# A two-part decoder on one core: first-block order of rounding, squares, tables, group merges and turned memory rows

## The chip, the cores and the metric

One NeuronCore of a Trainium2 chip runs the whole program. The metric is the device time of one execution in microseconds; the median of three runs of the kernel before is 2056.19 us (2055.5 to 2057.44). Five engines work side by side: TensorE (matmuls, PE in the rows; its weight loads are PEld), VectorE (DVE), ScalarE (ACT), GpSimd (POOL) and SyncE (SP), which issues most transfers. They meet only at semaphores.

## What is computed

256 tokens of width 1024, all in float32, pass through a first part of two blocks and a second part of four layers. The change lies in the first part and at the first layer of the second. Cut to what matters:

```python
for l in range(2):                                   # first part
    h = rms_norm(x, norm_gain[l])
    cols = h @ w_in[l]                               # 1024 -> many columns
    if l == 0:   # three groups of dilated attention (8 heads each), merged by softmax of their log-denominators
        q, k = rotary(rms_norm(q) * q_gain, cos, sin), rotary(rms_norm(k) * k_gain, cos, sin)
        alpha = softmax(stack([lse0, lse1, lse2]))
        mix = sum(alpha[g] * out[g] for g in range(3))
    else:        # gated linear scan with lower bounds from a softmax over lb_logits
        mix = hgrn2(cols, lower_bounds)
    kv = rms_norm(mem, mem_gain[l]) @ w_mem_kv[l]    # 256 memory rows, 4 heads
    mem_out = softmax(q_mem @ k_mem.T * scale) @ v_mem
    x = x + (concat([mix, mem_out]) * silu(gate)) @ w_out[l]
# second part: gated linear attention, latent attention, convolution, gated linear attention;
# the latent attention uses rotary tables of its own (other positions), each layer has an MLP and a gate
```

## The kernel before

`plan()` writes the whole order of work out by hand as a list of steps (`add(kind, ...)`), and `build()` walks that list once for each engine. So each engine executes its share of every step in the order of the list, and a step that waits holds up all that stands behind it on that engine.

**Weights** come as units of 128 x 2048 floats (1 MB), numbered in the order of use, through a ring of four slots. SyncE issues unit n when the subtraction of unit n - 4 is done (L862 to L864), the constants being issued ahead of unit 4. For float32 accuracy each unit is split in two: ScalarE writes `whi`, a rounded copy (L1256), VectorE writes `wlo` = raw - whi (L1563). TensorE multiplies three times (L908): hi x hi, hi x lo, lo x hi. ScalarE's copy runs three units ahead of the use, VectorE's subtraction two. A projection to 512 columns takes two units and 48 matmuls of 512 columns.

**Turned rows.** TensorE turns four 128 x 128 tiles into a bank (L1084), ScalarE writes the rounded copy (L1376), VectorE the rest (L2049), which frees the bank. There are two such banks. The products need the turned rows of h (X) or of y and of the memory (Y) as their other operand.

**First block.** Units 0 and 1 give the values of the memory, 2 and 3 its keys, 4 and 5 the memory's queries; then six times v, q and k of four heads (units 6 to 41), three groups for each half `hq` of the heads; units 42 to 47 are the gates, 48 to 53 the output product with its six chunks of rows (u = 0 to 5: 0 and 1 need heads 0 to 3, 2 and 3 heads 4 to 7, 4 and 5 the memory's part of y). After a projection of q or k ScalarE squares and copies both banks (L1298, L1265), VectorE reduces, takes the root and multiplies with scale and gain (L1666 to L1675), and turns by the angles (L1691 to L1702). The four heads of a quad go through a pipeline of slots between projections: T (turn q and k, L1005; copy by ScalarE, L1403), S (scores, L1026; mask and maximum on VectorE, L1842; exponential on ScalarE, L1410), PT (turn, L1034; copy L1856), PV (L1049; copy L1866). `combine` computes the weights of the three groups and then merges their outputs: 8 multiplications (L2105) and 16 multiply-adds (L2109). `ymul` (L2122) multiplies a chunk of y with its gate. `memgain` (`gained`, L1627) multiplies the memory rows by their gain, `xnorm` (`norm`) normalises x for the second block. `init` computes the rotary tables of the first block and the lower bounds, `mlatab` (L2191 to L2199) those of the latent attention; both need a sine or an exponential of ScalarE.

**Second block.** Units 54 and 55 are the memory's values, 56 and 57 its keys, 58 and 59 its queries, 60 onwards the second block's own projections. X holds the turned memory rows up to unit 57 and the turned x from unit 58.

The order of the steps around the change, as `plan()` has it before:

```python
add("memgain", layer=0); turn_x("mg", "Y"); add("first_units"); add("scales", what="mem")
...  # values, keys, queries of the memory: units 0 to 5
add("init"); add("mlatab")
...  # six rounds of v, q, k; combine(hq=0) after the fifth; the gates with turns of y; drain()
```

## Time and profile before

| what | us |
|---|---|
| median of three runs | 2056.19 |
| the profiled execution | 2057.1 |
| its span | 2055.3 |
| TensorE busy in it | 1908.8 |
| VectorE busy | 1207.5 |
| ScalarE busy | 910.0 |
| GpSimd busy | 593.1 |

The span is the time from the first to the last instruction of the profiled execution; the rest of its time lies around it. A row of the timeline gives the start in us, the length in us, the engine, the line, the operation, what it writes and reads, how many instructions are merged in it, and in brackets the idle time of the engine before it and who ended it.

### The profile page before, as it was taken

How to read it: one execution, taken by the hardware profiler on the slowest of the kernel's cores; microseconds unless marked ns; L12 is line 12 of the kernel's file. 1: busy time of each engine (PE TensorE's matmuls, PEld its weight loads, DVE VectorE, ACT ScalarE, POOL GpSimd, SP SyncE). 2: the span in 40 equal slices, each digit the busy share in tenths (PEclk: the TensorE clock that was granted, in tenths of full speed). 3: DMA queues.
4: the chain of work that ended last, by engine and by line, in shares of the span. 5: the costliest groups of instructions: out<-in, count | busy, mean ns of one | idle time of the engine just before them, and what ended most of it. 6: DMA issues, size and time to landing. Idle time of an engine off the chain costs nothing.

```text
span 2055.3 us, 27371 instructions
## 1 busy us (share of the span) xinstructions
PE 1908.8 (93%) x11072; PEld 1678.5 (82%) x11072; DVE 1207.5 (59%) x2062; ACT 910.0 (44%) x981; POOL 593.1 (29%) x132
## 2 busy tenths in 40 slices
PE   6899989989888988999989999999999988989998
PEld 5688877779777877899778899889899977779996
DVE  6788787775977397332566522566522376863236
ACT  5555545345443343444354444443444434334442
POOL 0000000000000001787400688500487700037870
PEclk9999999999899999999999999999999999999999
DMA  7344434534332234455443455444655533164551
GB/s 291 123 145 143 178 130 144 195 142 150 103 124 97 110 117 155 164 198 190 145 162 137 182 179 192 183 156 163 221 180 188 186 124 140 62 222 171 189 199 44
DMA packets 53412, 324.94 MB, mean 158 GB/s; under 512 B 8480, under 2 KB 11936, under 8 KB 16064
## 3 DMA queue, kind: packets, MB, share of 16 engines
q1 hardware_dynamic: 45344, 310.10, 41.4%
q10 hardware_dynamic: 7968, 13.44, 2.0%
q8 instruction: 70, 1.15, 0.2%
q14 instruction: 30, 0.25, 0.0%
HBM read 322.47 MB, written 1.05 MB: 157 GB/s over the span
## 4 chain that ended last, share of the span: by engine, by line
PE 73%; DVE 20%; ACT 4%; issue 2%; DMA 0%; SPq 0%; DVEq 0%; ACTq 0%
PE project L908 41%; PE output L908 25%; DVE wlo L1563 3%; PE turn L1084 1%; ACT whi L1256 1%; DVE XTl L2049 1%; PE output L1026 1%; PE output L1049 1%; DVE arena L1675 1%; DVE tok L2257 1%; DVE arena L1901 1%; DVE arena L1903 1%; DVE arena L1927 1%; ACT XTh L1376 1%; PE turn L1005 1%
## 5 line engine op out<-in xcount | busy, mean ns | idle before, releaser
L876 POOL TENSOR_TENSOR wlo<-raw,whi 128x2048 fp32r<-128x2048 f32 x128 | 592.9, 4660 | 1415.0 <-ACT whi L1256 1398.1
L1256 ACT ACTIVATE whi<-raw 128x2048 fp32r<-128x2048 f32 x291 | 554.4, 1913 | 477.3 <-PE project L908 308.4
L908 PE MATMUL project<-XTh,whi 128*128 128x256 f32 x1488 | 427.0, 287 | 4.4 <-DVE XTl L2049 3.0
L908 PE MATMUL project<-XTh,wlo 128*128 128x256 f32 x1488 | 425.0, 286 | 0.0
L908 PE MATMUL project<-XTl,whi 128*128 128x256 f32 x1488 | 424.9, 286 | 0.0
L2285 DVE TENSOR_TENSOR arena<-arena 128x512 f32<-128x512 f32 x64 | 143.2, 2271 | 462.0 <-ACT arena L1513 462.0
L1563 DVE TENSOR_TENSOR wlo<-raw,whi 128x2048 fp32r<-128x2048 f32 x163 | 376.6, 2323 | 39.0 <-ACT whi L1256 38.7
L908 PE MATMUL output<-whi,YTh 128*128 128x512 f32 x736 | 291.7, 396 | 13.2 <-DVE YTl L2049 11.4
L908 PEld LDWEIGHTS project<-XTh,whi 128*128 128x128 f32 x1488 | 290.0, 195 | 7.4 <-DVE XTl L2049 4.9
L908 PEld LDWEIGHTS project<-XTh,wlo 128*128 128x128 f32 x1488 | 289.9, 195 | 1.0
L908 PEld LDWEIGHTS project<-XTl,whi 128*128 128x128 f32 x1488 | 289.6, 195 | 0.0
L908 PE MATMUL output<-wlo,YTh 128*128 128x512 f32 x736 | 289.6, 393 | 0.0
L908 PE MATMUL output<-whi,YTl 128*128 128x512 f32 x736 | 289.1, 393 | 0.0
L908 PE MATMUL project<-whi,XTh 128*128 128x512 f32 x624 | 256.2, 411 | 12.7 <-DVE wlo L1563 9.3
L908 PE MATMUL project<-whi,XTl 128*128 128x512 f32 x624 | 246.0, 394 | 0.0
L908 PE MATMUL project<-wlo,XTh 128*128 128x512 f32 x624 | 246.0, 394 | 0.0
L908 PEld LDWEIGHTS output<-whi,YTh 128*128 128x128 f32 x736 | 140.2, 190 | 42.5 <-DVE YTl L2049 12.0
L908 PEld LDWEIGHTS output<-whi,YTl 128*128 128x128 f32 x736 | 139.9, 190 | 30.0
L908 PEld LDWEIGHTS output<-wlo,YTh 128*128 128x128 f32 x736 | 140.1, 190 | 27.6
L908 PEld LDWEIGHTS project<-whi,XTh 128*128 128x128 f32 x624 | 119.4, 191 | 41.5 <-DVE wlo L1563 12.3
L908 PEld LDWEIGHTS project<-whi,XTl 128*128 128x128 f32 x624 | 118.9, 190 | 26.3
L908 PEld LDWEIGHTS project<-wlo,XTh 128*128 128x128 f32 x624 | 119.4, 191 | 23.6
(245 smaller groups left out, 2104.7 us busy)
## 6 DMA issues: line engine op xcount, KB each, us to landing
raw<-in_units SPq DMA_DIRECT2D x291, 1024.0 KB, 4.8
arena<-in_ln_g ACTq DMA_DIRECT2D x8, 512.0 KB, 4.1
arena<-in_ln_b ACTq DMA_DIRECT2D x8, 512.0 KB, 4.9
arena<-in_mem_norm_gain ACTq DMA_DIRECT2D x2, 512.0 KB, 4.9
...
xres<-in_x SPq DMA_DIRECT2D x1, 1024.0 KB, 12.9
arena<-in_mem ACTq DMA_DIRECT2D x1, 1024.0 KB, 6.6
...
```

The costliest lines, as they stand in the source:

```text
L876: pool.tensor_tensor(wlo[:, slot, :], raw[:, slot, :], whi[:, slot, :], ALU.subtract).then_inc(lo_pool, 1)
L908: mm = pe.matmul(out, x if x_stationary else w, w if x_stationary else x, start=start and i == 0, stop=stop and i == 2, skip_group_check=True)
L1005: mm = pe.transpose(PT[hd["t"] % 2][:, x * P:(x + 1) * P], buf[:, h, jj * P:(jj + 1) * P], ident[:, :])
L1026: mm = pe.matmul(PQ[h2][:, h * S:h * S + n], qkT[:, h2, h * P:(h + 1) * P], qkT[:, h2, S:S + n], start=True, stop=True)
L1049: mm = pe.matmul(PQ[3][:, h * P:(h + 1) * P], pT[:, h2, x * P:(x + 1) * P], v, start=kt == 0, stop=kt == len(mine) - 1)
L1084: mm = pe.transpose(PT[f["t"] % 2][:, x * P:(x + 1) * P], s, ident[:, :])
L1256: act.activation(whi[:, slot, :], raw[:, slot, :], ACT.Copy).then_inc(hi_done, 1)
L1376: act.activation(dst[:, f["k"]:f["k"] + nk, f["h"] * P:(f["h"] + 1) * P], PT[t % 2][:, 0:nk * P].rearrange("p (k t) -> p k t", k=nk), ACT. ...
L1563: dve.tensor_tensor(wlo[:, slot, :], raw[:, slot, :], whi[:, slot, :], ALU.subtract).then_inc(lo_dve, 1)
L1675: ins = dve.scalar_tensor_tensor(out=v, in0=v, scalar=st[:, 24 + x:25 + x], in1=gain, op0=ALU.mult, op1=ALU.mult)
L1901: dve.tensor_tensor(QE[l % 2], q, Dx, ALU.mult).then_inc(dve_own, 1)
L2285: dve.tensor_tensor(hsq[:, b, :], relu[:, b, :], relu[:, b, :], ALU.mult).then_inc(hsq_ready, 1)
```

## The change

- The rounding of unit 0 stands between the two pairs of turns of the memory rows, those of units 1 and 2 and both subtractions behind them; the squares of the memory rows come after, and their scales within the first projection.
- `init` keeps the first block's tables and stands before the projection of the memory's queries. The lower bounds are a step `floors` of their own, before the memory keys of the second block. `mlatab` moves into the first projection of the second part, with the loads of its positions and constants, now on ScalarE's queue.
- `combine` keeps the weights only. The merges are steps `merge(hq, g)`: for hq = 0 groups 0 and 1 after the first unit of the last v projection, group 2 after the first unit of the last q projection; for hq = 1 between the units of the output product, whose order becomes 4, 5, 0, 1, 2, 3.
- The turns of y's chunk 0 move from inside the last gate projection to behind it.
- The gain multiplication of the memory rows (layer 1) comes after unit u = 1 of the output product, and their turns stand in two pairs before and between the halves of its tail (which is split into x = 0, 1 and x = 2, 3).
- `xnorm` stands between the two units of the second block's value projection, and the turns of x are split: the first four tiles of both halves between the key projection's units, the others behind it.
- In a slot ScalarE does the stage T before the others.

The diff, cut to what the text speaks of:

```diff
+            if xs[0] == 0:
+                units.extend((w, "Q", v, 0) for v in (u, u + 1))
+            m = len(units) - 2
+            add("tail", n=m, ahead=False, **f)
+            add("ahead", n=m + (xs[0] > 0), on="sv")
...
     add("memgain", layer=0)
-    turn_x("mg", "Y")
-    add("first_units")
-    add("scales", what="mem")
-    vg = project(("w_mem_kv", 0), 512, "v", src="M", par=0, between=lambda: add("xgain"))
+    turn("mg", 0, 0, "Y", 0)
+    turn("mg", 0, 1, "Y", 4)
+    add("first_units", s=(0,), v=())
+    turn("mg", 1, 0, "Y", 0)
+    turn("mg", 1, 1, "Y", 4, late=True)
+    add("first_units", s=(1, 2), v=(0, 1))
+    add("squares", what="mem")
+    vg = project(("w_mem_kv", 0), 512, "v", src="M", par=0,
+                 between=lambda: (add("scales", what="mem"), add("xgain")))
...
     project(("w_mem_kv", 0), 0, "qk", src="M", gain=7, rot=False, dst="k", between=lambda: turn_tok_half(1))
+    add("init")
     project(("w_in_a", 0), 9216, "qk", gain=6, rot=False, dst="q")
-    add("init")
-    add("mlatab")
     quad("mem", vg, par=0, g=3)
...
     for hq in range(2):
         for g in range(3):
             col = g * 1024 + hq * 512
-            vg = project(("w_in_a", 0), 6144 + col, "v", par=par)
-            project(("w_in_a", 0), col, "qk", gain=g, rot=True, dst="q")
+            last = hq == 1 and g == 2
+            vg = project(("w_in_a", 0), 6144 + col, "v", par=par, between=(lambda: merge(0, 0, 1)) if last else None)
+            project(("w_in_a", 0), col, "qk", gain=g, rot=True, dst="q", between=(lambda: merge(0, 2)) if last else None)
             project(("w_in_a", 0), 3072 + col, "qk", gain=3 + g, rot=True, dst="k")
...
     project(("w_in_a", 0), 9728, "gate", buf="A", between=lambda: turn_y(2))
     add("ymul", chunk=0, layer=0, second=0)
-    project(("w_in_a", 0), 9728 + 512, "gate", buf="A", between=lambda: turn_y(0))
+    project(("w_in_a", 0), 9728 + 512, "gate", buf="A")
+    for h in range(H2):
+        turn("y", h, 0, "Y", 0, late=True)
     drain()
 
     g, one, tail = begin_output(("w_out_a", 0), 1536)
     add("combine", hq=1, quads=(4, 5, 6))
+    add("load", what="mem")
+    one(4, first=True)
+    merge(1, 0, 1)
+    one(5)
+    merge(1, 2)
     add("ymul", chunk=1, layer=0, second=0)
-    add("load", what="mem")
-    one(0, first=True)
-    add("memgain", layer=1)
-    one(1)
-    one(4)
+    one(0, whole=True)
     for h in range(H2):
         turn("y", h, 1, "Y", 4, late=True)
     add("load", what="b")
-    one(5)
-    tail(2)
-
-
-    turn_x("tok", "X")
+    one(1)
+    add("memgain", layer=1)
+    turn("tok", 0, 0, "X", 0)
+    turn("tok", 0, 1, "X", 4)
+    tail(2, 0, 1)
+    turn("tok", 1, 0, "X", 0)
+    turn("tok", 1, 1, "X", 4)
+    tail(2, 2, 3)
+
     add("qpost", g=g, post="resid", src_n=n["src"])
-    add("xnorm", layer=1)
-    vg = project(("w_mem_kv", 1), 512, "v", par=2)
-
-    def turn_tok():
-        turn_x("tok", "X")
-
-    project(("w_mem_kv", 1), 0, "qk", gain=1, rot=False, dst="k", before_vector=turn_tok)
+    vg = project(("w_mem_kv", 1), 512, "v", par=2, between=lambda: add("xnorm", layer=1))
+
+    def turn_tok(c):
+        turn("tok", 0, c, "X", 4 * c, late=c == 1)
+        turn("tok", 1, c, "X", 4 * c, late=c == 1, later=1 - c)
+
+    add("floors")
+    project(("w_mem_kv", 1), 0, "qk", gain=1, rot=False, dst="k", between=lambda: turn_tok(0),
+            before_vector=lambda: turn_tok(1))
...
-        project(w, 0, "fq", feature_major=True, scale=SCALE, second=1)
+        project(w, 0, "fq", feature_major=True, scale=SCALE, second=1, between=(lambda: add("mlatab")) if j == 0 else None)
...
+                if j == 0:
+                    load(posM.bitcast(I32), a["pos_row"].to_broadcast([P, S]), pos_in)
+                    load(small, a["c_small"], pos_in)
...
                 elif kind == "first_units":
-                    for n in range(AHEAD):
+                    for n in f["s"]:
                         hi(n, n, 1)
...
-                    for stage, i in f["stages"]:
+                    for stage, i in sorted(f["stages"], key=lambda x: x[0] != "T"):
...
+                elif kind == "merge":
+
+                    g = f["g"]
+                    dve.wait_ge(*last.at)
+                    for j in range(4):
+                        for h in range(H2):
+                            y = yA[:, h, (4 * f["hq"] + j) * P:(4 * f["hq"] + j + 1) * P]
+                            s = st[:, 32 + 8 * g + 2 * j + h:33 + 8 * g + 2 * j + h]
+                            if g == 0:
+                                dve.tensor_scalar(y, y, s, None, ALU.mult).then_inc(dve_own, 1)
+                                last.own()
+                            else:
+                                o = tok[:, g - 1, h * 512 + j * P:h * 512 + (j + 1) * P]
+                                dve.scalar_tensor_tensor(out=y, in0=o, scalar=s, in1=y, op0=ALU.mult, op1=ALU.add).then_inc(dve_own, 1)
+                                last.own()
+                    dve.wait_ge(*last.at)
                 elif kind == "ymul":
```

## Rows read from the trace of the kernel before

**Rows 1.** Page, chain that ended last: shares of the span by engine.
```profile
PE 73%; DVE 20%; ACT 4%; issue 2%; DMA 0%; SPq 0%; DVEq 0%; ACTq 0%
```

**Rows 2.** Timeline of TensorE, first 460 us: rows after long stops.
```profile
19.49 0.76 PE L908 MATMUL project<-whi,YTh 128*128 128x512 f32 x1 [4.90 <-DVE wlo L1563]
...
76.91 2.07 PE L1026 MATMUL output<-arena 128*128 128x256 f32 x4 [8.63 <-ACT arena L1403]
...
297.70 0.80 PE L908 MATMUL project<-whi,XTh 128*128 128x512 f32 x1 [4.75 <-DVE wlo L1563]
...
350.80 0.63 PE L1084 MATMUL turn<-ident,arena 128*128 128x128 f32 x4 [2.09 <-ACT arena L1403]
...
376.40 0.94 PE L1049 MATMUL output<-arena 128*128 128x128 f32 x6 [1.30 <-DVE arena L1856]
...
390.08 0.50 PE L908 MATMUL output<-whi,YTh 128*128 128x512 f32 x1 [1.82 <-DVE wlo L1563]
```

**Rows 3.** Windows of 24 matmuls, TensorE: window, length, busy (count), granted clock, DMA, GB/s.
```profile
78.98:86.09 7.11, 7.11 (x27) 0.77 0.79 303
87.83:93.33 5.50, 5.50 (x27) 1.00 0.20 48
...
351.43:358.53 7.10, 7.10 (x26) 0.76 0.37 113
```

**Rows 4.** Start: unit 0's transfer (issue to landing), then timelines of three engines.
```profile
raw<-in_units SPq DMA_DIRECT2D x1, 1024.0 KB, 8.1
...
15.12 3.70 ACT L1256 ACTIVATE whi<-raw 128x2048 fp32r<-128x2048 f32 x2
...
21.25 56.80 SPq L864 DMA_DIRECT2D raw<-in_units  x10
...
30.54 1.92 ACT L1256 ACTIVATE whi<-raw 128x2048 fp32r<-128x2048 f32 x1 [5.00 <-DMA raw<-in_units]
...
45.63 0.69 ACT L1298 ACTIVATE arena<-project,st 128x512 f32<-128x512 f32 x1 [1.39 <-PE project L908]
...
51.40 4.49 DVE L1563 TENSOR_TENSOR wlo<-raw,whi 128x2048 fp32r<-128x2048 f32 x2
```

**Rows 5.** Timeline of VectorE and ScalarE, tables and bounds.
```profile
62.28 0.16 DVE L1971 CAST st<-st 128x2 f32<-128x2 int32 x1
...
65.09 0.26 ACT L1362 ACTIVATE arena<-arena 128x64 f32<-128x64 f32 x1 [4.21 <-DVE arena L1616]
65.36 1.28 ACT L1366 ACT_TABLE_LOAD   x1
66.66 0.22 ACT L1366 ACTIVATE lbs<-lbs 128x16 f32<-128x16 f32 x1
...
67.63 0.29 DVE L2191 CAST arena<-arena 128x256 f32<-128x256 int32 x1
...
72.81 0.35 DVE L2199 TENSOR_SCALAR csM<-csM,arena 128x256 f32<-128x256 f32 x1 [0.70 <-ACT csM L1370]
```

**Rows 6.** Timeline of VectorE, first merge and what follows.
```profile
289.21 1.66 DVE L2105 TENSOR_SCALAR arena<-arena,st 128x128 f32<-128x128 f32 x8
290.90 4.42 DVE L2109 SCALAR_TENSOR_TENSOR arena<-tok,st,arena 128x128 f32<-128x128 f32 x16
...
305.63 0.56 DVE L1856 COPY arena<-output 128x384 f32<-128x384 f32 x1 [2.51 <-PE output L1034]
...
312.88 0.42 DVE L1866 COPY tok<-output 128x256 f32<-128x256 f32 x1 [3.54 <-PE output L1049]
```

**Rows 7.** Second part's start: a small load (issue to landing), then timelines.
```profile
arena<-in_gla_glr ACTq DMA_DIRECT2D x1, 64.0 KB, 2.3
...
690.12 0.60 ACT L1265 ACTIVATE arena<-project 128x512 f32<-128x512 f32 x1 [7.79 <-PE project L908]
...
695.63 0.49 DVE L2146 TENSOR_TENSOR YTl<-arena,YTh 128x128 fp32r<-128x128 f32 x2 [10.94 <-ACT YTh L1453]
```

**Rows 8.** Timeline of ScalarE, a slot of the gate stage.
```profile
349.19 0.40 ACT L1410 ACTIVATE arena<-arena,negm 128x128 f32<-128x128 f32 x1 [3.43 <-DVE negm L1848]
...
350.08 0.57 ACT L1403 ACTIVATE arena<-turn 128x512 f32<-128x512 f32 x1
```

**Rows 9.** TensorE's waits, 400 to 460 us (total, times, longest); then VectorE's timeline.
```profile
PE turn L1084 <- DVE XTl L2049: 3.1, 2, 1.8
PE project L908 <- DVE XTl L2049: 1.6, 2, 0.8
PE project L908 <- DVE wlo L1563: 1.5, 1, 1.5
...
443.01 1.29 DVE L2049 TENSOR_TENSOR XTl<-turn,XTh 128x512 fp32r<-128x512 f32 x2 [8.65 <-ACT XTh L1376]
...
454.19 4.49 DVE L1563 TENSOR_TENSOR wlo<-raw,whi 128x2048 fp32r<-128x2048 f32 x2
```

44 lines of the change are left out of this document (19 added, 25 removed).

## The prediction

> **What bounds the kernel now.** I read three views in this order. The chain that ended last gives TensorE 73% of the span and VectorE 20% [rows 1]: the time is TensorE's own work plus the places where it stands still. The timeline of TensorE with its idle times, read over the first 460 us (all that the diff touches but the angle tables of the second part), gives those places [rows 2]. The granted clock over equal groups of work gives the second part of the price: 24 matmuls take 5.50 us at 1.00 (2.4 GHz), and 7.10 and 7.11 us where the clock over them averages 0.76 and 0.77, so part of them ran at 1.2 GHz [rows 3]. The slow group is the one right after the stop of 2.09 us; the stops of 8.63 and 4.75 us are followed by such groups too, and the first matmul after 4.75 us takes 0.80 us, after 1.82 us only 0.50 [rows 2]. So a long stop costs its own length plus 1.6 us, a short one its own length.
>
> I number the 1 MB weight units as the kernel does. Each needs a rounding copy on ScalarE (1.9 us [rows 4]) and a subtraction on VectorE (2.3 us [rows 9]) before TensorE may use it.
>
> **The start.** TensorE begins at 19.49 [rows 2]. Before that ScalarE does two squares in front of the turned tiles, and unit 0's rounding starts only at 15.12, though its transfer landed 8.1 us after its issue at 2.1, so at 10.2 [rows 4]. The change rounds unit 0 between the two pairs of turns. Working forward: turned copies until 9.7, rounding 10.2 to 12.1, second pair of copies to 13.3, the rests on VectorE to 14.1, then unit 0's subtraction to 16.4. TensorE would begin about 3.0 us earlier. But 13.4 us later it wants the value bank freed, by a ScalarE copy that stands in the queue behind the rounding of unit 4. That rounding waited 5.00 us for its transfer and ran from 30.54 [rows 4]. The constants ahead of unit 4 on the SP queue stay, except one of 128 KB, some 0.4 us. The copy thus ends near 32.6, and TensorE goes on at 32.65 where before it went on at 33.5. **The 3.0 us shrink to 0.85.** The stop that takes their place is about 1.9 us, between the one of 1.82 without and the one of 2.09 with a lowered clock; I take it as without and keep 1.6 us for the range.
>
> **Tables out of the way.** Now VectorE does both tables and the bounds in one run from 62.28 to 73.2, ScalarE waits 4.21 us and then again for it [rows 5], the roundings and TensorE stand behind, and TensorE stops 8.63 us [rows 2]. The change puts only the first table ahead of the projection of q. It is 2.8 us on VectorE (62.28 to 65.09 [rows 5]) plus 0.35 us for the sine. Queued behind it: on VectorE unit 6's subtraction; on ScalarE, which waits for VectorE's angles, unit 7's rounding and then the square and copy of q's first bank. The k projection ends at 45.6 now, where ScalarE takes up its square [rows 4], and would end at 44.75. From there: 5.9 us to the end of VectorE's normalisation (as now, 45.6 to 51.5, the next subtraction from 51.40 [rows 4]), 2.8 table, 0.35 sine, 1.9 rounding, 1.3 square and copy, which is 56.95. Unit 6 began at 56.51 before, so this point is 0.45 us *later* and the start's gain is used up. What is late next: q's normalisation ends near 64, just before its first turn at 65.2. I find no further wait. Gain here: 8.63, plus 1.0 for the four score matmuls after the stop (2.07 us [rows 2], half of it at the full clock), plus 1.6 for the next 24, less 0.45: **10.8 us**.
>
> Each sine also switches ScalarE's table: 1.28 us, and the load starts before the wait, under cover. The rows show nothing after the load: the one at 65.36 ends at 66.64 and the exponential runs from 66.66 [rows 5]. The Trainium skill, *ScalarE: Activation LUTs*, section "What ACT_TABLE_LOAD costs", puts a switch at about 2.66 us, with a drain of 1.38 us. By that the first block would lose another 1.4 us at unit 7's rounding; the rest of the sum goes without it.
>
> **Second table.** It moves into the first projection of the first gated layer of the second part, behind one subtraction. VectorE needs 5.5 us for it (67.63 to 73.16 [rows 5]) where it sat idle 10.94 us [rows 7]; ScalarE, which would wait about 4.3 us for it, is idle there 7.79 us until the next bank is full, 690.12 [rows 7]. Queued behind on VectorE is one subtraction, needed some 7 us later. Nothing on the path: 0. Its two transfers go out on ScalarE's queue, about 0.45 us each, before a rounding that waits for TensorE in any case. If the cover were gone it would cost at most 5.5 us. The bounds' own step (about 2.2 us, after unit 57's subtraction) has unit 58's subtraction behind it, due more than 5 us later: 0.
>
> **First merge in pieces.** Now 6.1 us of merges (1.66 and 4.42 [rows 6]) stand before unit 38's subtraction, and TensorE stops 4.75 us [rows 2]. The weights' own chain (about 2.4 us ahead of 289.21) stays. With the merges moved, unit 38 is ready at 291.5, before its use at 292.95. Then VectorE does 3.9 us of merge, unit 39, and only at 298.0 the scores that TensorE finished at 292.5. Their exponential ends at 299.7; TensorE, through with unit 38 at 298.4, and with a turn, wants it at 298.75. **New wait 1.0 us**, without a loss of clock. The remaining 2.2 us go behind the next scores. VectorE's two idle stretches here, 2.51 and 3.54 us [rows 6], are together as long as the merges, so unit 42 finds nothing late. Gain: 4.75 + 1.6 - 1.0 = **5.4 us**.
>
> **Turned copy ahead of the exponential.** In the gate stage TensorE waits 2.09 us [rows 2] for a turned copy at 350.08, which stands behind an exponential that waited for VectorE [rows 8]. The turn itself was over by 347.3. Taking it first ends that stop and its slow group: 2.09 + 1.6 = **3.7 us**. In the other slots it changes the order of two ScalarE steps that nobody waits for: 0.
>
> **The output product and the second memory block.** Here stand 1.30 and 1.82 us [rows 2], 3.1 and 1.6 (two stops of each kind, around the turned rows) and 1.5 us [rows 9], 9.3 together. The first shrinks to about 0.5, as the turns of y now run while VectorE copies. Chunks 4 and 5 go first, so unit 50's subtraction comes behind the weights' chain alone: 5 us early. The merges (3.9, 2.2) and the gate product (1.4) end at about 388, one microsecond before the turn of chunk 1. The memory rows are then turned between products, where TensorE has 5.5 us of other matmuls after each pair; their gain multiplications end 0.6 us before they are wanted, the narrowest cover in this stage. The norm's 7.5 us run beside the value projection. The second turning is split by halves, so the rests of the first pair are done under unit 57. New is this: from the k projection's end to unit 60's subtraction it takes 13.4 us (1.9 to the first rest, and from 443.01 to 454.19 less one pair, plus 2.3 [rows 9]), while TensorE has only one pair of turns and two units, 11.9 us. **Wait 1.5 us** at unit 60. Gain: 9.3 - 0.5 - 1.5 = 7.3, and some 0.6 us for six restarts of the matmul pipe: **7.9 us**.
>
> **The sum.** 10.8 + 5.4 + 3.7 + 7.9 = 27.8 us. The profiled execution has a span of 2055.3 and a time of 2057.1, so 1.8 us lie around the span; it would become 2027.5 and 2029.3. The median of the runs shown, 2056.19, is 0.9 below the profiled one: **2028.4 us**, a ratio of 0.986. After unit 60 nothing on the path is changed.
>
> **The rivals.** *(a) The new short waits lower the clock, or VectorE becomes the bound.* TensorE now arrives earlier at places where VectorE works without a pause. Three new stops (1.9 at the value bank, 1.0 at unit 38's scores, 1.5 at unit 60) with 1.6 us each cost 4.8 us more: 2033.2. For it: the first of them is near 2 us. Against: the stop of 1.82 us. *(b) The start's gain survives.* If unit 4 lands earlier because its slot is asked for earlier, up to 2.1 us more come through, and unit 6 moves along since its chain hangs on the k projection: 2026.3. Against: the SP queue issues unit 4 at 21.25 [rows 4], after its constants, and not when slot 0 came free at 19.3. *(c) The merges come back.* If the merges in the g2 projections hold up q's or k's normalisation by their whole length, the first merge's 5.4 us are lost and no more: 2033.8. *(d) Slower than before:* the position row and the small constants now land late. VectorE's angles wait for them, the next subtraction stands behind, and TensorE wants that unit about 697. A landing before 690 costs nothing; each microsecond after that costs one, so 34 us late (724) makes the kernel slower by 0.2%. Its issue is near 662 and the first of the other small loads there landed after 2.3 us [rows 7], so I give it almost nothing. *(e) It doesn't do what it says:* if TensorE's stops are only moved, as where VectorE's total work sets the time, the gain is that of the tables alone, 11 us: 2045. Against it: VectorE's idle stretches stand beside the stages concerned [rows 6, 7].
>
> **Chances.** Forecast 0.62, (a) 0.14, (b) 0.08, (c) 0.08, (e) 0.04, a loss that I don't see but still faster 0.01, no change 0.015, slower 0.015 ((d) among it). The range 2022.5 to 2034.5 takes in (a), (b) and (c) with the unknown ends: 2.5 us for the two new waits if they don't come, and as much again for stops that I have mis-sized. Less than 0.2% (4 us) can't be told from no change here; faster 0.97, same 0.015, slower 0.015.
>
> **What would show it.** Right: TensorE's first matmul near 16.5 and a stop of some 2 us near 31; unit 6 near 57; no stop at 68 to 77 and scores near 69; a stop of 1 us instead of 4.75 after unit 38; none before the turns of y; one of 1.5 us at unit 60; granted clock 1.00 after each. Wrong: a stop over 2 us in any of these with a group at 0.8, a stop in the first gated layer near 660, or a difference in the spacing of the second part.

## The result and the profile after

The changed kernel takes **2029.45 us** (median of four runs, 2026.15 to 2030.73) beside 2056.82 us for the kernel before in the same session (2055.5 to 2057.9). The ratio is 0.9865, with a 95% interval from 0.9848 to 0.9882. The forecast was 2028.4 within 2022.5 to 2034.5. The profiled execution has a span of 2028.9 us and a time of 2030.67.

The first 460 us of TensorE's timeline show nearly all of it. Columns are start, length, engine, line, operation, and in brackets the idle time before the row with what ended it. Lines of the changed kernel are 27 to 33 higher in this region (L908 is now L935, L1563 is L1593). It answers [rows 2].

```profile
16.31 0.76 PE L935 MATMUL project<-whi,YTh 128*128 128x512 f32 x1 [4.54 <-DVE wlo L1593]
...
31.46 0.47 PE L935 MATMUL project<-whi,YTh 128*128 128x512 f32 x1 [0.57 <-ACT arena L1292]
...
55.49 0.47 PE L935 MATMUL project<-whi,XTh 128*128 128x512 f32 x1 [1.09 <-ACT arena L1292]
...
98.66 0.47 PE L935 MATMUL project<-whi,XTh 128*128 128x512 f32 x1 [0.47 <-ACT arena L1292]
...
287.66 0.55 PE L1061 MATMUL output<-ident,arena 128*128 128x128 f32 x3 [1.13 <-ACT arena L1440]
...
354.21 0.94 PE L1076 MATMUL output<-arena 128*128 128x128 f32 x6 [0.43 <-DVE arena L1886]
...
409.36 0.47 PE L935 MATMUL project<-whi,XTh 128*128 128x512 f32 x1 [1.62 <-DVE XTl L2079]
...
428.27 0.50 PE L935 MATMUL project<-whi,XTh 128*128 128x512 f32 x1 [1.43 <-DVE wlo L1593]
```

The stops of 8.63, 4.75, 2.09 and 1.82 us are gone. What stands there now is short, and no slow group follows: the first matmul behind each stop at a weight unit takes 0.47 to 0.50 us, not 0.80. The granted clock over the stretches that begin at these stops is 1.00, where [rows 3] had 0.77 and 0.76 (columns as there).

```profile
31.46:37.00 5.54, 5.54 (x24) 1.00 0.59 231
...
67.41:71.00 3.59, 3.59 (x18) 1.00 1.01 420
287.66:293.00 5.34, 5.34 (x26) 1.00 0.93 370
...
409.36:415.00 5.64, 5.64 (x25) 1.00 0.32 135
428.27:434.00 5.73, 5.73 (x25) 1.00 0.80 296
```

Then something goes the other way. I use two marks in the code that the change left alone: the first turn in the scan of the second block (the last chunk's, the "scan turn" below), and the first matmul of the eighth scan level. Between them the changed kernel takes 43.1 us and the kernel before 39.2. First the changed kernel:

```profile
492.91 1.97 PE L1111 MATMUL turn<-ident,arena 128*128 128x128 f32 x8 [3.11 <-DVE arena L2155]
...
536.04 1.16 PE L1170 MATMUL output<-arena 128*128 128x128 f32 x8 [1.40 <-DVE arena L1938]
```

and the kernel before:

```profile
521.42 1.26 PE L1084 MATMUL turn<-ident,arena 128*128 128x128 f32 x8 [3.10 <-DVE arena L2122]
...
560.63 2.08 PE L1143 MATMUL output<-arena 128*128 128x128 f32 x8 [1.40 <-DVE arena L1908]
```

So in these two profiles the gain is 28.5 us at the scan turn (521.42 - 492.91), 24.6 at the eighth level, and 26.4 at the end of the span (2055.3 - 2028.9). Is the loss of 3.9 us a price of the change, or does it come from elsewhere? That became the main question for the experiments, next to the forecast's own terms.

### The profile page after: what moved, and what is told of

It is laid out like the page before. It is cut to its first block, busy times and chain, and to the rows that moved or that the text cites. A ratio compares the mean times of both kernels' runs of the same rounds, so it can differ in the third digit from the quotient of the medians.

```text
span 2028.9 us, 27379 instructions
## 1 busy us (share of the span) xinstructions
PE 1907.0 (94%) x11072; PEld 1679.5 (83%) x11072; DVE 1206.5 (59%) x2062; ACT 910.5 (45%) x981; POOL 593.2 (29%) x132
## 4 chain that ended last, share of the span: by engine, by line
PE 73%; DVE 20%; ACT 3%; issue 3%; SPq 1%; DMA 0%; DVEq 0%; ACTq 0%
PE project L935 40%; PE output L935 26%; DVE wlo L1593 3%; PE turn L1111 1%; ACT whi L1283 1%; DVE XTl L2079 1%; DVE arena L1705 1%; DVE tok L2290 1%; PE output L1076 1%; SPq L866 1%; PE output L1053 1%; DVE arena L1931 1%; DVE arena L1933 1%; DVE arena L1957 1%; DVE st L2272 1%
## 5 line engine op out<-in xcount | busy, mean ns | idle before, releaser
L935 PE MATMUL project<-XTh,whi 128*128 128x256 f32 x1488 | 426.4, 287 | 4.1 <-DVE XTl L2079 3.1
L935 PE MATMUL project<-XTh,wlo 128*128 128x256 f32 x1488 | 424.4, 285 | 0.0
L935 PE MATMUL project<-XTl,whi 128*128 128x256 f32 x1488 | 424.2, 285 | 0.0
L1593 DVE TENSOR_TENSOR wlo<-raw,whi 128x2048 fp32r<-128x2048 f32 x163 | 376.9, 2322 | 38.8 <-ACT whi L1283 38.0
L935 PE MATMUL output<-whi,YTh 128*128 128x512 f32 x736 | 291.4, 396 | 11.4 <-DVE YTl L2079 11.4
L935 PEld LDWEIGHTS project<-XTh,whi 128*128 128x128 f32 x1488 | 289.3, 194 | 7.2 <-DVE XTl L2079 4.9
L935 PEld LDWEIGHTS project<-XTh,wlo 128*128 128x128 f32 x1488 | 289.1, 194 | 1.0
L935 PE MATMUL output<-wlo,YTh 128*128 128x512 f32 x736 | 289.2, 393 | 0.0
L935 PEld LDWEIGHTS project<-XTl,whi 128*128 128x128 f32 x1488 | 288.9, 194 | 0.0
L935 PE MATMUL output<-whi,YTl 128*128 128x512 f32 x736 | 288.9, 392 | 0.0
L935 PE MATMUL project<-whi,XTh 128*128 128x512 f32 x624 | 255.1, 409 | 8.9 <-DVE wlo L1593 4.5
L935 PE MATMUL project<-whi,XTl 128*128 128x512 f32 x624 | 245.4, 393 | 0.0
L935 PE MATMUL project<-wlo,XTh 128*128 128x512 f32 x624 | 244.9, 392 | 0.0
L935 PEld LDWEIGHTS output<-whi,YTh 128*128 128x128 f32 x736 | 140.2, 190 | 39.9 <-DVE YTl L2079 12.0
L935 PEld LDWEIGHTS output<-whi,YTl 128*128 128x128 f32 x736 | 139.7, 190 | 29.8
L935 PEld LDWEIGHTS output<-wlo,YTh 128*128 128x128 f32 x736 | 140.0, 190 | 27.6
L935 PEld LDWEIGHTS project<-whi,XTh 128*128 128x128 f32 x624 | 118.9, 191 | 37.1 <-DVE wlo L1593 8.5
L935 PEld LDWEIGHTS project<-whi,XTl 128*128 128x128 f32 x624 | 118.2, 189 | 26.0
L935 PEld LDWEIGHTS project<-wlo,XTh 128*128 128x128 f32 x624 | 118.7, 190 | 23.3
```

The costliest lines, as they stand in the source:

```text
L935: mm = pe.matmul(out, x if x_stationary else w, w if x_stationary else x, start=start and i == 0, stop=stop and i == 2, skip_group_check=True)
L1593: dve.tensor_tensor(wlo[:, slot, :], raw[:, slot, :], whi[:, slot, :], ALU.subtract).then_inc(lo_dve, 1)
```

## The experiments

The first four kernels ran together, then the next four, then the last four; the kernel before ran beside them each time (2056.36, 2056.86 and 2056.66 us). Two theories stand over all of them for the lost 3.9 us. **A**: the moments at which TensorE's clock falls and comes back around the scan turn differ by chance. **B**: the change, by its timing or its order, keeps the clock low.

### The changed kernel again

No edit.

> The changed kernel once more, unaltered. It asks about the first scan levels of the second block: from the first turn of y's third chunk (492.9) to the eighth level's matmuls (536.0) the profiled changed kernel takes 43.1 us, the kernel before 39.2 us, although nothing there was edited. Theory A (chance: after the stops there the clock comes back at another moment in each execution): another execution gives another length, between 39 and 44, and single times spread over some 4 us. Theory B (the change itself lowers the clock there, by arriving at it in another state): 43 again, within 0.5. Everything up to unit 60 (428.3) repeats within 0.3 us in either case.

Measured: 2029.47 us (2024.19 to 2030.23), ratio 0.9861 [0.9845, 0.9878]. Unit 60 at 428.4, scan turn at 493.02, from there to the eighth level 42.9 us. The single length spoke for B, though the four times spread over 6 us, which theory A had expected (some 4 us).

### The old start

```diff
-    turn("mg", 0, 0, "Y", 0)
-    turn("mg", 0, 1, "Y", 4)
-    add("first_units", s=(0,), v=())
-    turn("mg", 1, 0, "Y", 0)
-    turn("mg", 1, 1, "Y", 4, late=True)
-    add("first_units", s=(1, 2), v=(0, 1))
     add("squares", what="mem")
+    turn_x("mg", "Y")
+    add("first_units", s=(0, 1, 2), v=(0, 1))
+    add("scales", what="mem")
```

> The changed kernel with the start of before: squares ahead of the turned copies, all three roundings behind them, the scales ahead of the first projection. Theory (the start is limited by unit 4's transfer, and its gain reaches unit 6 because that unit hangs on the end of the memory's k projection): first matmul at 19.5 in place of 16.3, but unit 2 at 33.5 in place of 31.5 and unit 6 at 57.5 in place of 55.5: 2.0 us of the 3.2 come through, unit 60 at 430.3. Rival (as I predicted: only 0.85 comes through): unit 2 at 32.3, unit 60 at 429.1. Rival 2 (all comes through): unit 60 at 431.5. Time about 2 us over the changed kernel.

Measured: 2029.43 us (2026.55 to 2031.76), ratio 0.9872 [0.9856, 0.9889]. The first matmul is back at 19.61, unit 2 starts at 33.97, unit 6 at 58.00, unit 60 at 430.85 and the scan turn is at 495.50, 2.4 us later than in the mean of the changed kernel's four profiles (493.1). That lies between the theory (2.0) and rival 2 (all 3.2); the rival (0.85) is out. Yet the median is the same; in the profiled execution the stretch behind the scan turn takes 39.1 us. A median of four runs can't show what the start is worth. The trace can. It also shows why my forecast of the start was too low. Three timelines, of ScalarE's rounding of unit 4, in the changed kernel, in this one, and in the next (old tables), whose position row is back on the SP queue:

```profile
28.83 1.92 ACT L1283 ACTIVATE whi<-raw 128x2048 fp32r<-128x2048 f32 x1 [1.90 <-DMA raw<-in_units]
```

```profile
28.93 1.92 ACT L1279 ACTIVATE whi<-raw 128x2048 fp32r<-128x2048 f32 x1 [3.27 <-DMA raw<-in_units]
```

```profile
20.89 0.43 SPq L867 DMA_DIRECT2D arena<-in_pos_row  x1
21.37 21.69 SPq L893 DMA_DIRECT2D raw<-in_units  x6
...
29.76 1.91 ACT L1285 ACTIVATE whi<-raw 128x2048 fp32r<-128x2048 f32 x1 [2.72 <-DMA raw<-in_units]
```

With the old start but without the row, unit 4 is ready at 28.93, as early as with the new start. With the new start and the row it is ready at 29.76, and in the two profiles of the kernel before (old start and row) at 30.54 [rows 4] and 30.39. Over the eleven profiles without the row this start lies between 28.76 and 29.18. So the row on the queue costs 0.6 to 1.0 us of landing with the new start (29.76 against 28.76 to 29.18), and 1.5 to 1.6 with the old one (30.39 and 30.54 against 28.93), though its issue takes only 0.43 us. The traffic shows it too: from 24 to 26 us the transfers move 153 GB/s in this one profile with the new start and the row and 186 and 192 in the kernel before, but 269 to 330 in all profiles without the row. Without the row the moment at which slot 0 comes free plays no part (28.93 against 28.83). Why it costs more with the old start stays open.

### The old tables and bounds

```diff
-    add("init")
     project(("w_in_a", 0), 9216, "qk", gain=6, rot=False, dst="q")
+    add("init")
+    add("floors")
+    add("mlatab")
...
+                load(posM.bitcast(I32), a["pos_row"].to_broadcast([P, S]), pos_in)
```

(Not shown: at their new places `floors`, `mlatab` and the two small loads go.)

> The changed kernel with both tables and the bounds again behind the projection of the memory's queries, and the loads as before. Theory (the stop is the price, all else stays): TensorE stops 8.6 us before the first scores of memory, then runs a group of 24 at a clock under 0.8; 8.6 + 1.0 + 1.6 less the 1.1 us stop at unit 6 = 10.1 us more at unit 12 (98.7 to 108.8) and at unit 60 (428.3 to 438.4). Rival (later stops of VectorE absorb part of it, since it could work ahead during the stop): under 6 us at unit 60. The first layer of the second part shows no difference in either.

Measured: 2041.73 us (2040.74 to 2042.16), ratio 0.9929 [0.9912, 0.9945]. TensorE's timeline has the long stop back:

```profile
75.78 2.08 PE L1055 MATMUL output<-arena 128*128 128x256 f32 x4 [8.61 <-ACT arena L1432]
...
109.46 0.47 PE L937 MATMUL project<-whi,XTh 128*128 128x512 f32 x1 [0.50 <-ACT arena L1294]
```

Unit 12 starts at 109.46 and not at 98.66: 10.8 us, up to 0.9 of them from the row's effect on unit 4 (unit 2 starts at 32.40 and not at 31.46). The expectation was 10.1; the rival, under 6, is out. The stop's clock is in it. The windows from 75.78 to 80.00 and from 80.00 to 84.00 show 0.50 and 0.94, and 1.00 behind. The scan turn is 10.6 us later (503.70), and the stretch behind it takes 41.6 us, a value between the two seen so far. What the first gated layer of the second part shows is told below, at the second table.

### The old first merge

```diff
-            vg = project(("w_in_a", 0), 6144 + col, "v", par=par, between=(lambda: merge(0, 0, 1)) if last else None)
-            project(("w_in_a", 0), col, "qk", gain=g, rot=True, dst="q", between=(lambda: merge(0, 2)) if last else None)
+            vg = project(("w_in_a", 0), 6144 + col, "v", par=par)
+            project(("w_in_a", 0), col, "qk", gain=g, rot=True, dst="q")
...
+                merge(0, 0, 1, 2)
```

> The changed kernel with the three merges of the first half back in one piece behind their weights. Theory: the stop of 4.75 us ahead of unit 38 and its slow group come back and the stops of 0.23 and 1.13 us go: unit 42 5.1 us later (310.5 to 315.6), unit 60 the same 5.1 us later (433.4). Rival (VectorE's whole work bounds this stretch, so that the merges cost their 6.1 us wherever they stand): under 2 us.

Measured: 2033.87 us (2031.19 to 2036.16), ratio 0.9887 [0.987, 0.9903]. The stop is back, the new one of 1.13 is not there:

```profile
285.60 0.79 PE L936 MATMUL project<-whi,XTh 128*128 128x512 f32 x1 [4.96 <-DVE wlo L1594]
```

Unit 42 starts at 316.53 and not at 310.48, 6.05 us later: 4.96 less 1.13 is 3.8 of them. I put the remaining 2.2 down to the clock, which stood at 0.50 over the 4.4 us from 285.60. The expectation was 5.1; the rival, under 2, is out. The scan turn is 5.9 later (498.98), the stretch behind it 42.9.

### Turned copies in the old order

```diff
-                    for stage, i in sorted(f["stages"], key=lambda x: x[0] != "T"):
+                    for stage, i in f["stages"]:
```

> The changed kernel, with the turned copy of attention's result no longer taken first among the copies of an output group: ScalarE copies in the order in which the pieces stand, as before the change. Forecast by the prediction's step (turned copy first, 3.7): TensorE's stop of about 2.1 us at the first transpose of the attention rows comes back, with the slower group of matmuls behind it at a granted clock below 1.00, and unit 57 and unit 60 start 3.7 us later than in the changed kernel (409.4 and 428.3 there); median about 3.5 later. Rival: the copy was late only because of the merges, which now stand elsewhere; then the stop stays gone and the times are those of the changed kernel within 0.5. On the clock in the second block's scan levels (turn of chunk 2 to level 8, 43 us in the changed kernel, 39 with the start undone): theory A, it depends on when the stop falls and not on the change: any value between 39 and 44; theory B, the change's later parts cause it: 43.

Measured: 2032.98 us (2031.27 to 2034.98), ratio 0.9889 [0.9871, 0.9907]. The stop of 2.09 is back:

```profile
333.99 0.63 PE L1111 MATMUL turn<-ident,arena 128*128 128x128 f32 x4 [2.09 <-ACT arena L1433]
```

But the slow group is not. TensorE's window behind it:

```profile
334.00:350.00 16.00, 16.00 (x86) 1.00 0.32 109
```

The same stop, to the hundredth of a microsecond, had a clock of 0.76 behind it in [rows 3], and a lowered one in the second profile of the kernel before too (0.68 over the first 4 us). So its price is 2.1 us and a restart, or 1.6 more with the slow group, and which of them is paid is not a matter of the stop's length. With one profile of this kernel, whether chance or something else in the order decides at this stop isn't shown. From unit 42 to the output product this kernel takes 46.75 us and the changed kernel 44.4, so undoing the order costs 2.3 here. Units 57 and 60 are 2.9 us later (3.7 expected), the scan turn 2.7 (495.83), some 0.4 of it from before unit 42. The rival (no stop) is out. The stretch behind the scan turn takes 39.1 us.

### The old order of the output product

```diff
-    one(4, first=True)
-    merge(1, 0, 1)
-    one(5)
-    merge(1, 2)
+    merge(1, 0, 1, 2)
     add("ymul", chunk=1, layer=0, second=0)
     one(0, whole=True)
+    one(4, first=True)
...
-    turn("tok", 0, 0, "X", 0)
-    turn("tok", 0, 1, "X", 4)
-    tail(2, 0, 1)
-    turn("tok", 1, 0, "X", 0)
-    turn("tok", 1, 1, "X", 4)
-    tail(2, 2, 3)
+    one(5)
+    tail(2)
+    turn_x("tok", "X")
```

(Not shown: the turns of y and the second load now stand between chunks 1 and 5. The order of the chunks is 4, 0, 1, 5, where the kernel before had 0, 1, 4, 5, so this is near the old order and not the same. The turns of y's chunk 0 stay behind the last gate projection here; no run moves them back.)

> The changed kernel with the output product and its memory rows scheduled as before the change: the last merge in one piece, token groups 4, 0, 1, 5 in the old order, the tail whole, and the turns of the memory block's rows behind all of it. Forecast by the prediction's step (9.3 removed less 0.5 and 1.5 of new waits and 0.6 kept, for this and for the second block's order together): TensorE's stops of 1.8, 1.3 and 0.5 us in the output product come back, unit 57's stop of 1.62 us goes since nothing turned is still on its way, and the normalisation stands in front of the value projection. Unit 60 starts 4 to 6 us later than in the changed kernel (428.3), so near 433; median 4 to 5 later. Rival: the three stops came from the merges in one piece of the first block alone, and the order in the output product is worth under 1.5 us. On the clock in the second block's scan levels: theory A any value between 39 and 44 us; theory B 39, since the turns that the change put in front are gone.

Measured: 2036.97 us (2035.69 to 2039.85), ratio 0.9906 [0.9887, 0.9926]. TensorE's timeline:

```profile
368.17 0.50 PE L929 MATMUL output<-whi,YTh 128*128 128x512 f32 x1 [2.12 <-DVE wlo L1587]
...
393.36 1.23 PE L1105 MATMUL turn<-ident,tok 128*128 128x128 f32 x8 [1.35 <-DVE XTl L2073]
395.40 0.79 PE L929 MATMUL project<-whi,XTh 128*128 128x512 f32 x1 [0.81 <-DVE XTl L2073]
...
415.93 0.47 PE L929 MATMUL project<-whi,XTh 128*128 128x512 f32 x1 [1.62 <-DVE XTl L2073]
...
434.84 0.50 PE L929 MATMUL project<-whi,XTh 128*128 128x512 f32 x1 [1.44 <-DVE wlo L1587]
```

Unit 60 is 6.6 us later (434.84), a little above the expected 4 to 6; the scan turn 6.4. The stops shown ahead of unit 57 sum to 4.3 us. Another 1.4 is the clock behind the pair of 1.35 and 0.81, 0.57 over 4 us:

```profile
395.00:399.00 4.00, 3.60 (x10) 0.57 0.00 0
```

From 395.40 the next 24 matmuls take 6.98 us; behind the same pair in the first profile of the kernel before (at 417.34) they take 5.58 us, and in the second profile of the kernel before 7.02. I had expected the 1.3 us ahead of the output product (376.40 in [rows 2]) back, and it stayed at 0.43: that gain is not this order's, and the move of the turns of y's chunk 0, which stays, is what the prediction gave it to. I had expected unit 57's 1.62 us to go, and it did not. It belongs to the order of the second memory block and not to the output product. The stretch behind the scan turn takes 39.2 us.

### The old order of the second memory block

```diff
-    vg = project(("w_mem_kv", 1), 512, "v", par=2, between=lambda: add("xnorm", layer=1))
+    add("xnorm", layer=1)
+    vg = project(("w_mem_kv", 1), 512, "v", par=2)
...
-    project(("w_mem_kv", 1), 0, "qk", gain=1, rot=False, dst="k", between=lambda: turn_tok(0),
-            before_vector=lambda: turn_tok(1))
+    project(("w_mem_kv", 1), 0, "qk", gain=1, rot=False, dst="k", before_vector=lambda: turn_x("tok", "X"))
```

> The changed kernel with the second memory block in the old order: the normalisation of the memory rows ahead of the value projection, and all turns of the token rows behind the key projection. The output product stays as the change has it. Forecast: of the two stops that the changed kernel shows there (1.62 us at unit 57 for a turned copy, 1.43 at unit 60 for a rounded half) both go or shrink, and those of before at the key projection and at the turns (1.5, 1.6, 0.8) come back; unit 60's counterpart, the first query unit, starts 1.0 to 1.6 us later than 428.3. Rival: VectorE has the same work ahead of unit 57 whichever way it is ordered, so the sum is the same within 0.5 us.

Measured: 2029.43 us (2027.36 to 2032.92), ratio 0.9865 [0.9847, 0.9883]. The two stops of the changed kernel go, and the two around the turned rows come back, 2.61 us in place of 3.05. The third that I expected, 1.5 us at unit 56 [rows 9], does not, so its removal is not this part's work:

```profile
415.28 1.22 PE L1107 MATMUL turn<-ident,tok 128*128 128x128 f32 x8 [1.79 <-DVE XTl L2075]
417.32 0.79 PE L931 MATMUL project<-whi,XTh 128*128 128x512 f32 x1 [0.82 <-DVE XTl L2075]
```

By its stops the old order is 0.4 us better, not 1.0 to 1.6 worse. But here the clock falls behind them, as the windows show:

```profile
415.00:419.00 4.00, 2.90 (x12) 0.68 0.00 0
419.00:423.00 4.00, 4.00 (x10) 0.50 0.45 137
423.00:427.00 4.00, 4.00 (x18) 0.97 0.30 125
```

That costs some 2.8 us (2.4 later at the next common unit in spite of 0.4 less of stops), so the scan turn is 2.5 us late (495.61). In the kernel before, the same pair of stops at 443.85 and 445.89 had a clock of 1.00 on both sides. So this part of the change is worth nothing by its stops, and some 3 us in executions in which the clock falls behind the old ones. It did so in this one profile and in neither of the two of the kernel before. The stretch behind the scan turn takes 42.9 us.

### Two waits removed: units 57 and 59

The changed kernel's stop at 409.36 is not one of those I forecast. The profile shows what is wrong with it. VectorE's timeline in the changed kernel around it:

```profile
404.73 2.29 DVE L1593 TENSOR_TENSOR wlo<-raw,whi 128x2048 fp32r<-128x2048 f32 x1
407.97 1.29 DVE L2079 TENSOR_TENSOR XTl<-turn,XTh 128x512 fp32r<-128x512 f32 x2 [0.95 <-ACT XTh L1406]
...
416.90 1.29 DVE L2079 TENSOR_TENSOR XTl<-turn,XTh 128x512 fp32r<-128x512 f32 x2 [7.64 <-ACT XTh L1406]
```

TensorE waits until 409.36 for rests of the tiles 0 to 3, which the code turned just before; unit 57 itself reads tiles 4 to 7. The wait comes from `wait_turned`, which waits for every turned pair in flight unless it is marked `late`, and this pair is not (`late=c == 1`). And VectorE then stands idle for 7.64 us, and does the rests of the next pair ahead of unit 59's subtraction although both could wait in the other order.

```diff
                 elif kind == "proj":
-                    wait_turned("Y" if f["src"] == "M" else "X", whole=f["u"] == 1)
+                    if f["n"] != 57:
+                        wait_turned("Y" if f["src"] == "M" else "X", whole=f["u"] == 1)
...
         if before_vector is not None:
+            add("ahead", n=m, on="v")
             before_vector()
         if tag in ("qk", "fq"):
-            add("ahead", n=m, on="sv")
+            add("ahead", n=m, on="s" if before_vector is not None else "sv")
```

> The changed kernel with two waits removed by their cause. First, unit 57 (the first value unit of the second memory block) no longer waits for the turned pair of tiles 0 to 3: it reads tiles 4 to 7 alone, and that pair's copies are waited for by the unit that reads them. Second, the subtraction that makes unit 59's low half of its weights goes to VectorE ahead of the rests of the turned token rows and not behind them. Forecast, since TensorE waits 1.62 us at unit 57 (for VectorE's rests of tiles that this unit does not read) and 1.43 us at unit 60 (for VectorE's low half): both stops go, unit 60 starts 3.05 us earlier than 428.3, at 425.3, and the median is 2 to 4 lower than the changed kernel's 2029.5. Rival one: VectorE is late for the next thing too, and the 1.62 comes back at unit 58 or 60; then the gain is 1.4 or less. Rival two: the stops go and the scan levels' clock comes back at another moment, so that the median moves by anything between -6 and +1.

Measured: **2023.97 us** (2022.45 to 2027.29), ratio 0.9846 [0.9827, 0.9866]. Both stops are gone and none takes their place up to the scan turn, which is at 489.60, 3.5 us earlier than in the changed kernel's runs. Rival one is out. The half microsecond beyond 3.05 is two restarts. Matmuls of 512 columns last 0.39 us here and start 0.23 apart, so they overlap by 0.16. At unit 60 of the changed kernel the last one starts at 426.45, the next at 428.27 and the one behind at 428.61: 2.16 us where two spacings are 0.46, so 1.70 for a stop of 1.43. A restart thus costs 0.27 there. At unit 57 it takes 2.65 us from the turn's start (406.71) to the first matmul, and 0.79 in this kernel: 0.24 beyond the 1.62. The median is 5.5 us lower, more than the 2 to 4 expected: the rest lies behind the scan turn (39.5 us to the eighth level and 1526.7 to the last matmul, as short as the shortest of the changed kernel's four). That is what rival two allowed.

### Four waits removed

The edit of the run before, and:

```diff
-    project(("w_mem_kv", 0), 0, "qk", src="M", gain=7, rot=False, dst="k", between=lambda: turn_tok_half(1))
     add("init")
+    project(("w_mem_kv", 0), 0, "qk", src="M", gain=7, rot=False, dst="k", between=lambda: turn_tok_half(1))
...
-            vg = project(("w_in_a", 0), 6144 + col, "v", par=par, between=(lambda: merge(0, 0, 1)) if last else None)
-            project(("w_in_a", 0), col, "qk", gain=g, rot=True, dst="q", between=(lambda: merge(0, 2)) if last else None)
+            vg = project(("w_in_a", 0), 6144 + col, "v", par=par, between=(lambda: merge(0, 0)) if last else None)
+            project(("w_in_a", 0), col, "qk", gain=g, rot=True, dst="q", between=(lambda: merge(0, 1)) if last else None)
...
-    project(("w_in_a", 0), 9728, "gate", buf="A", between=lambda: turn_y(2))
+    project(("w_in_a", 0), 9728, "gate", buf="A", between=lambda: (merge(0, 2), turn_y(2)))
```

> The changed kernel with four waits removed by their cause: the two of the run before (unit 57 waits no longer for tiles that it does not read; unit 59's low half is made ahead of the turns' rests), then the groups' merge in three pieces at three places (one in the value projection, one in the query projection, one in the second gate projection) and the constants of the scan set up ahead of the first memory key projection and not behind it. Forecast: unit 57's 1.62 and unit 60's 1.43 gone (3.5 at the turn of the last chunk, as the run before showed), the stops of 1.10 behind the merge and 1.09 at unit 6 gone too; the turn of the last chunk at 487.2 us (492.9 in the changed kernel); median 2021.5, range 2019 to 2025, against the changed kernel's 2029.5 and the 2024.0 of the run before. Rival: VectorE's queue is full around the merge and the 1.1 comes back at another unit; then the turn of the last chunk is at 488.5 and the median near 2023.

Measured: **2022.66 us** (2022.38 to 2024.99, five runs), ratio to the kernel before 0.9839 [0.9826, 0.9853]. TensorE's timeline has no stop over 0.5 us between these two:

```profile
31.52 0.47 PE L936 MATMUL project<-whi,YTh 128*128 128x512 f32 x1 [1.38 <-ACT arena L1294]
...
486.68 1.26 PE L1112 MATMUL turn<-ident,arena 128*128 128x128 f32 x8 [3.06 <-DVE arena L2157]
```

The scan turn is at 486.68 (487.2 expected), 6.4 us earlier than in the changed kernel and 2.9 earlier than in the run before. The median is 1.2 above the expected 2021.5 and inside its range. Of the changed kernel's ten times (2024.19 to 2030.73) one lies below this kernel's slowest; against the run before the times overlap widely (2022.45 to 2027.29), and there only the trace tells them apart.

### Two more executions of the changed kernel, one of the kernel before

No edits; one execution each, with its profile.

> The changed kernel once more, for the moments at which TensorE's clock falls and comes back in one execution. From the turn of the last chunk of the second block to the eighth scan level, the ten profiles so far take 39.1, 39.1, 39.2, 39.2, 39.5, 41.6, 42.3, 42.9, 42.9 and 43.1 us, the changed kernel's own two 43.1 and 42.9. Theory A, it is chance from execution to execution: one of two more profiles of the changed kernel has the clock fall behind the turn's start and back at 1.00 within 8 us of it, and the stretch takes 39 to 40. Theory B, it belongs to this kernel's timing: 43 in both. Up to that turn all else within 0.3 us of the first profile.

> As the run before: the changed kernel again. Theory A: the scan levels' stretch takes 39 to 40 us in this or in the run before; theory B: 43 in both.

> The kernel before, once more, for the same: its one profile took 39.2 us from the turn of the last chunk (521.4) to the eighth level. Theory A: chance decides, 39 to 43 here. Theory B: 39.2 again. All stops up to there as in the first profile within 0.1 us, and so the turn of the last chunk at 521.4 within 0.5, unless the clock falls at other stops too.

Measured: the changed kernel took 2028.5 and 2026.78 us. Its scan turn was at 493.12 and 493.30, and the stretch behind it took **39.1 and 39.5 us**, in the same kernel that twice took 43. The kernel before took 2059.66 us, with the scan turn at 522.55 and 39.2 us behind it. I had expected the scan turn within 0.5 us of 521.4; it came 1.1 later, 0.6 of that ahead of the first scores, the most of the rest behind the stops of 8.64 and 2.09. For the changed kernel that is theory A; B's "43 in both" is out. The windows show where the 4 us are. First the changed kernel's first profile, then the third, from 4 us ahead of the scan turn:

```profile
488.91:492.91 4.00, 0.90 (x4) 0.98 0.18 31
492.91:496.91 4.00, 1.97 (x8) 0.50 0.69 252
496.91:500.91 4.00, 3.71 (x16) 0.50 0.61 246
...
504.91:508.91 4.00, 4.00 (x10) 0.50 0.00 0
508.91:512.91 4.00, 4.00 (x19) 0.88 0.70 262
```

```profile
489.12:493.12 4.00, 0.92 (x5) 1.00 0.18 39
493.12:497.12 4.00, 1.50 (x8) 0.61 0.68 244
497.12:501.12 4.00, 3.67 (x16) 0.54 0.61 246
501.12:505.12 4.00, 3.85 (x25) 1.00 0.00 0
```

TensorE has been idle for 3.1 us and its clock falls to 0.50 (1.2 GHz) around the turn in both. Behind the turn it stands still for another 2.3 and 2.8 us and is then busy nearly without a pause in both; in the third profile the clock is back at about 501, in the first near 510. What decides between them stays open. In the four profiles with 42.9 to 43.1 us the clock had fallen ahead of the turn (0.91 to 0.98 in the 4 us before it), while in all of those with 39.1 or 39.2 it fell only behind it. But in two profiles it fell ahead (0.87 in the changed kernel's fourth, 0.86 with two waits removed) and the stretch took 39.5. So the moment of the fall alone doesn't settle it.

A second place shows the same more sharply. Where the second part begins, all fourteen profiles have the same two stops, 1.42 or 1.43 and 0.81 or 0.82 us, and then the same work up to a stop of 0.78. In nine it takes 24.06 to 24.08 us. In five it takes 25.49 to 25.52, and there the first matmul takes 0.58 us and not 0.39. One of the two profiles of the kernel before is among the five (25.51, the other 24.08), and one of the four of the changed kernel. So the same kernel and the same stops give either length: a price of nothing or 1.4 us, by execution.

### All profiles side by side

Read from the fourteen traces; us. The last column but one runs from the scan turn to the start of the last matmul. The last is the median or, for single executions, the one time.

| kernel | scan turn at | to the eighth level | to the last matmul | time |
|---|---|---|---|---|
| before | 521.42 | 39.2 | 1529.0 | 2056.8 |
| before, again | 522.55 | 39.2 | 1530.4 | 2059.7 |
| changed | 492.91 | 43.1 | 1531.0 | 2029.5 |
| changed, again | 493.02 | 42.9 | 1530.5 | 2029.5 |
| changed, third | 493.12 | 39.1 | 1528.7 | 2028.5 |
| changed, fourth | 493.30 | 39.5 | 1526.7 | 2026.8 |
| old start | 495.50 | 39.1 | 1525.0 | 2029.4 |
| old tables | 503.70 | 41.6 | 1531.2 | 2041.7 |
| old first merge | 498.98 | 42.9 | 1530.5 | 2033.9 |
| turned copies in old order | 495.83 | 39.1 | 1528.7 | 2033.0 |
| old output product | 499.51 | 39.2 | 1531.5 | 2037.0 |
| old second memory block | 495.61 | 42.9 | 1530.6 | 2029.4 |
| two waits removed | 489.60 | 39.5 | 1526.7 | 2024.0 |
| four waits removed | 486.68 | 39.2 | 1529.0 | 2022.7 |

Up to the scan turn the four profiles of the changed kernel agree within 0.4 us, so an edit's worth is read there to a fraction of a microsecond, unless the clock falls behind a stop that the edit brings back. The two of the kernel before, which has such stops, differ by 1.1. Behind it all kernels execute the same stages (the one edit there, the moved second table, included) and take 1525.0 to 1531.5 us, with no order by kernel.

## Why the prediction was right, point by point

**The sum.** Forecast 27.8 us up to unit 60, measured 28.7 there (456.95 to 428.27). By the medians the gain is 27.4, by the mean of all ten times of the changed kernel (2028.4) it is 28.4. The forecast gain of 27.8 lies between them. That the time was met to 1 us is in part luck: the start gave 1.5 us more than I had it, and in the profiled execution 2.3 us were lost again between unit 60 and the end of the span (28.7 there, 26.4 at the end), where I had nothing and where one kernel's executions differ by 4 us. Undoing the six parts one at a time moves the scan turn by 2.4, 10.6, 5.9, 2.7, 6.4 and 2.5 us from the mean of the four profiles (493.1), 30.5 together. The kernel before, which has all of them undone and y's turns of chunk 0 and the chunks' order as well, is 28.3 and 29.5 later. The parts nearly add up; the clock behind the old second block's stops (2.8) and behind the old output product's (1.4) is in the sum, and the first profile of the kernel before has neither.

**The start: a term too low, by a mis-sized transfer.** I let the 3.0 us shrink to 0.85 at unit 2 and to nothing at unit 6. Measured: first matmul 16.31 (16.4 forecast), unit 2 at 31.46 (32.65), unit 6 at 55.49 (56.95). What failed is the step "except one of 128 KB, some 0.4 us". I priced the position row by its issue. Its effect is on the landing of what is issued behind it: unit 4's rounding started 1.7 us earlier, at 28.83 where it was 30.54, and with it unit 2, 2.6 us after that rounding's start in all four profiles (31.46 to 31.70). Of the 1.7 us, the row's absence alone gives 1.5 to 1.6 with the old start; put back beside the new start, it takes 0.6 to 1.0. This is rival (b)'s result, 1.5 us more at unit 12, but not its mechanism: without the row, slot 0's release has no part in it, since the old start gets unit 4 as early.

The stop at unit 2 was 0.57 to 1.71 us in the changed kernel's four profiles, not 1.9. Its length says nothing of the landing: it varies with how long TensorE is slow at the start. Its first matmuls start 0.43 us apart, as they do elsewhere at 0.50, and then 0.23, from 21.57 on in the first profile and from 19.43 in the third. The granted clock reads 1.00 over all of it, so that column alone would have hidden this. From the key projection's end on, my chain held: 12.2 us forecast to unit 6, 11.9 measured (43.55 to 55.49).

**The tables: right.** 10.8 forecast; 10.8 by undoing them, of which up to 0.9 is the row's share. Unit 6 waits 1.09 us, as the chain through VectorE's table said. ScalarE's timeline at the first sine in the changed kernel:

```profile
46.64 1.28 ACT L1392 ACT_TABLE_LOAD   x1
52.13 0.26 ACT L1392 ACTIVATE arena<-arena 128x64 f32<-128x64 f32 x1 [4.20 <-DVE arena L1646]
52.29 1.91 ACT L1283 ACTIVATE whi<-raw 128x2048 fp32r<-128x2048 f32 x1
```

The load stands ahead of the wait and is over 4.2 us before the sine; the rounding follows the sine without a gap, so unit 7's rounding doesn't lose the 1.4 us. The Trainium skill (*ScalarE: Activation LUTs*, section "What ACT_TABLE_LOAD costs") gives 1.38 us of drain per switch. Here a drain behind the load would lie under the wait and couldn't be seen; in [rows 5], where no wait follows, the exponential starts 0.02 us behind the load, and there is none. As these rows have it, such a switch costs 1.28 us, and nothing where a longer wait follows the load.

**The second table: right, 0.** In the second part ScalarE waits for it and TensorE does not: its timeline has no stop between the projection's first matmul at 655.62 and 679.69. That is 24.07 us, and the second profile of the kernel before, without the table there, takes 24.08. With the old tables it is 25.51, as in the first profile of the kernel before: the clock's 1.4 us behind the two stops ahead of it, and not the table. It answers [rows 7].

```profile
658.04 1.28 ACT L1400 ACT_TABLE_LOAD   x1
662.80 0.63 ACT L1400 ACTIVATE csM<-csM 128x512 f32<-128x512 f32 x1 [3.47 <-DVE csM L1646]
664.55 0.60 ACT L1292 ACTIVATE arena<-project 128x512 f32<-128x512 f32 x1 [1.12 <-PE project L935]
```

After it ScalarE is idle again for 1.12 us before its next bank is full. So rival (d), slower than before by a late position row, had no ground: VectorE takes the row up at 658.28 without waiting for it.

**The first merge: right, with the new wait.** 5.4 forecast, 5.1 measured at unit 42 (17.4 there less 12.3 at unit 36), and 6.05 by undoing it. The new wait was put at 1.0 us and is 1.13. Taking it away by a third piece elsewhere gave back its length and a restart (1.3 to 1.5 us between unit 12 and the output product), so it was the merges' own and no bound by VectorE.

**Turned copy first: the mechanism right, the size a matter of the clock.** 3.7 forecast, 3.9 measured between unit 42 and the output product (22.2 less 17.4 less the 0.9 of the shorter stop there), 2.3 by undoing it. The stop is worth 2.1 and a restart; the other 1.6 were there in both profiles of before and not in the profile with the stop put back.

**Output product and second memory block: nearly right, for a reason partly wrong.** 7.9 forecast, 7.4 measured at unit 60. The wait of 1.5 us at unit 60 came as 1.43. But that the rests of the first pair are done "under unit 57" was false: unit 57 waits 1.62 us for them, though it doesn't read them. I had followed the data and not the code's wait. By its stops the new order of the second block is 0.4 us worse than the old one. The output product carries the term, 6.4 to 6.6 us by undoing it (1.4 of them the clock), together with the 0.9 at the turns of y. The six restarts at 0.6 us, 0.1 each, were mis-sized too: one measures 0.2 to 0.3.

**The rule of 1.6 us behind a long stop.** I charged it to stops of 4.75 and 8.63 us and of 2.09, and not to those under 2. Measured when put back: behind 4.96 it is 2.2, behind 8.61 the clock is at 0.50 for some 4 us, behind 2.09 nothing, where both profiles of before lose some 1.6, behind 1.79 and 0.82 2.8, where both lose nothing. Behind 1.35 and 0.81 it is 1.4 when put back, nothing in one profile of before and 1.4 in the other, and there the next stop, 1.49 in the first (unit 56), shrinks to 0.04 and takes it up: the scan turn pays nothing. That is one place with both outcomes in one unaltered kernel, and the pair of 1.42 and 0.81 in the second part is another. So behind stops of this length it is a chance and not a price. Rival (a) rested on that chance; none of the new stops paid it in any profile of the changed kernel.

**Rivals (c) and (e)** fell: no normalisation was held up by the merges, and the stops' removal carried through to the scan turn whole.
